# The gated sum of the experts joins the residual on two engines, and the closing norm is written anew

## What is computed

```python
combine = ...                              # [tokens, 8], two entries of a row are not zero
out = jnp.zeros_like(t)
for e in range(N_EXPERTS):
    out = out + combine[:, e:e + 1] * swiglu(t, w_gate[e], w_up[e], w_down[e])
x = x + g_f * out
# at the very end
xf * lax.rsqrt(jnp.mean(xf * xf, axis=-1, keepdims=True) + NORM_EPS) * g
```

## Time and profile before

| what | us |
|---|---|
| median of 3 runs | 1572.42 |
| range of these runs | 1570.97 to 1575.75 |
| the profiled execution, whole time | 1572.48 |
| its span on the core, from first to last instruction | 1570.7 |
| outside of the span | 1.8 |

### The profile page before, as it was taken

The page is one execution under the profiler, slowest core; times in us unless marked ns, Lnnn a source line. Parts: engine busy times, 40 slices in busy tenths (PEclk is TensorE's granted clock), DMA queues, the critical chain, the costliest instruction groups (busy, mean ns, idle before and its releaser), DMA issues.

```text
span 1570.7 us, 19868 instructions
## 1 busy us (share of the span) xinstructions
PE 1471.8 (94%) x7238; PEld 1200.2 (76%) x7239; DVE 1240.2 (79%) x1722; ACT 915.9 (58%) x1202; POOL 5.1 (0%) x17
## 2 busy tenths in 40 slices
PE   7999999997999998988899998959999999999995
PEld 5888888885788887866788887747778878877883
DVE  6767889768667888777777886795888888898887
ACT  6656564547556654465433333554776787777674
POOL 0000000000000000000000000000000000000000
PEclk9999999999999999999999998979999999999997
DMA  9654448873345467643567784312588889888882
GB/s 350 235 222 154 173 168 302 318 270 134 134 164 192 167 227 269 241 161 111 186 254 267 252 320 172 108 54 81 200 323 306 312 302 338 307 312 325 303 315 92
DMA packets 53416, 358.16 MB, mean 228 GB/s; under 512 B 6096, under 2 KB 7120, under 8 KB 12640
## 3 DMA queue, kind: packets, MB, share of 16 engines
q1 hardware_dynamic: 52736, 354.77, 60.9%
q0 software_dynamic: 176, 2.13, 0.4%
q10 hardware_dynamic: 432, 0.30, 0.1%
HBM read 356.13 MB, written 1.05 MB: 227 GB/s over the span
## 4 chain that ended last, share of the span: by engine, by line
PE 68%; DVE 17%; ACT 7%; issue 6%; DMA 1%; PEldq 0%; DVEq 0%; PEld 0%; ACTq 0%; SPq 0%
PE ps L437 21%; PE ps L439 20%; PE ps L438 20%; DVE wlo L1527 6%; ACT whi L1055 3%; PE ps L916 2%; PE ps L595 1%; DVE tok L2224 1%; PE ps L646 1%; PE ps L529 1%; DVE attn_scratch L1856 1%; DMA raw<-stream_dram 1%; DVE tok L1775 1%; ACT attn_scratch L1245 1%; DVE tok L1709 1%
## 5 line engine op out<-in xcount | busy, mean ns | idle before, releaser
L1527 DVE TENSOR_TENSOR wlo<-raw,whi 128x2048 fp32r<-128x2048 f32 (+2 forms) x304 | 651.3, 2165 | 144.1 <-ACT whi L1055 131.0
L1055 ACT ACTIVATE whi<-raw 128x2048 fp32r<-128x2048 f32 (+2 forms) x304 | 547.5, 1819 | 233.2 <-PE ps L439 228.3
L437 PE MATMUL ps<-whi,xhi 128*128 128x512 f32 (+3 forms) x1360 | 536.5, 394 | 19.5 <-DVE wlo L1527 9.4
L439 PE MATMUL ps<-whi,xlo 128*128 128x512 f32 (+3 forms) x1360 | 524.0, 385 | 0.0
L438 PE MATMUL ps<-wlo,xhi 128*128 128x512 f32 (+3 forms) x1360 | 523.8, 385 | 0.0
L437 PEld LDWEIGHTS ps<-whi,xhi 128*128 128x128 f32 x1360 | 258.2, 190 | 81.0 <-DVE wlo L1527 13.0
L439 PEld LDWEIGHTS ps<-whi,xlo 128*128 128x128 f32 x1360 | 257.9, 190 | 52.3
L438 PEld LDWEIGHTS ps<-wlo,xhi 128*128 128x128 f32 x1360 | 258.5, 190 | 47.0
L437 PE MATMUL ps<-whi,ahi 128*128 128x512 f32 x440 | 177.9, 404 | 5.2 <-DVE wlo L1527 5.1
L439 PE MATMUL ps<-whi,alo 128*128 128x512 f32 x440 | 174.1, 396 | 0.0
L438 PE MATMUL ps<-wlo,ahi 128*128 128x512 f32 x440 | 173.2, 394 | 0.0
(11 more groups left out here) (286 smaller groups left out, 1179.9 us busy)
## 6 DMA issues: line engine op xcount, KB each, us to landing
raw<-stream_dram SPq DMA_DIRECT2D x317, 1024.0 KB, 5.1
raw<-stream_dram SPq DMA_DIRECT2D x32, 512.0 KB, 4.3
attn_scratch<-toep_dram POOLq DMA_DIRECT2D x1, 2048.0 KB, 9.5
raw<-stream_dram SPq DMA_DIRECT2D x2, 528.0 KB, 4.4
h<-x_dram SPq DMA_DIRECT2D x2, 512.0 KB, 4.8
y<-tok SPq DMA_DIRECT2D x2, 512.0 KB, 2.7
head_scratch<-w_s_dram SPq DMA_DIRECT2D x1, 512.0 KB, 14.2
head_scratch<-vg_dram SPq DMA_DIRECT2D x1, 512.0 KB, 11.2
```

Of the source, the lines that this page charges most:

```text
L437: pe.matmul(o, xh, wh, start=start, stop=False)
L439: return pe.matmul(o, xl, wh, start=False, stop=stop)
L1055: act.activation(whi[:, q % SPL, 0:w], raw[:, s % RAW, 0:w], ACT.Copy).then_inc(sem("hi_done"), 1)
L1527: dve.tensor_tensor(wlo[:, q % SPL, 0:w], raw[:, s % RAW, 0:w], whi[:, q % SPL, 0:w].bitcast(F32), ALU.subtract).then_inc(sem("lo_done"), 1)
```

## The change

- POOL gets a queue behind its table. When the last residual before the experts is added (`h_added` at 14) it loads the closing norm's weights into `gates[:, 0]`, a gate's place that is free from there on. When `y_added` is at eight it multiplies `macc` by the gate and adds it to `h`, tile by tile, four instructions of 128 x 1024.
- `scatter` and `add_expert` go through the tiles outside and the halves inside, where it was the other way.
- Behind the loop `add_gated` takes the place of `add_expert`: for each tile, two instructions of 128 x 512 that make PSUM * `comb` * gate, and one of 128 x 1024 that adds this to `h`. DVE waits for POOL (`others_in`) before it.
- DVE multiplies `h` by the norm's weights while ACT squares; then one small instruction for both tiles at each step of the root; then DVE scales the left halves and ACT the right halves, and SP stores four pieces of 128 x 512.

```diff
-            sp.wait_ge(sem("y_copied"), 2 * NE + 1)
-            sp.wait_ge(sem("y_psum"), 2 * (2 * NE + 1))
-            sp.dma_start(TC[:, 0, :], fg_in.to_broadcast([P, D])).then_inc(sem("fg_landed"), 16)
             for t in range(NT):
-                sp.wait_ge(sem("y_ready"), t + 1)
-                sp.dma_start(out[0, t * P:(t + 1) * P, :], TA[:, t, :]).then_inc(sem("stored"), 16)
-            sp.wait_ge(sem("stored"), 16 * NT)
+                for n, done in enumerate(("out_left", "out_right")):
+                    sp.wait_ge(sem(done), t + 1)
+                    sp.dma_start(out[0, t * P:(t + 1) * P, n * W:(n + 1) * W], TA[:, t, n * W:(n + 1) * W]).then_inc(sem("stored"), 16)
+            sp.wait_ge(sem("stored"), 2 * 16 * NT)
...
+            g.wait_ge(sem("h_added"), 7 * NT)
+            g.dma_start(gates[:, 0, :], fg_in.to_broadcast([P, D])).then_inc(sem("fg_landed"), 16)
+            g.wait_ge(sem("y_added"), NE)
+            for t in range(NT):
+                g.tensor_tensor(macc[:, t, :], macc[:, t, :], gates[:, 1, :], ALU.mult).then_inc(sem("others_gated"), 1)
+                g.wait_ge(sem("others_gated"), t + 1)
+                g.tensor_tensor(h[:, t, :], macc[:, t, :], h[:, t, :], ALU.add).then_inc(sem("others_in"), 1)
...
-            stats(h)
+            act.activation(st[:, 26:27], ones[:, 0:1], ACT.Sqrt)
+            act.wait_ge(sem("h_added"), T.up("h_added", NT))
+            for t in range(NT):
+                act.activation(TA[:, t, :], h[:, t, :], ACT.Square, accum_out=st[:, t:t + 1]).then_inc(sem("sq"), 1)
+            act.wait_ge(sem("ms"), T.up("ms"))
+            act.activation(st[:, 4:6], st[:, 2:4], ACT.Sqrt).then_inc(sem("rms"), 1)
+            act.wait_ge(sem("end_rinv"), 1)
+            for t in range(NT):
+                act.activation(TA[:, t, W:D], macc[:, t, W:D], ACT.Copy, scale=st[:, 28 + t:29 + t]).then_inc(sem("out_right"), 1)
...
+            def add_gated(i):
+                for t in range(NT):
+                    dve.wait_ge(sem("y_psum"), T.up("x_y"))
+                    for n in range(2):
+                        c = slice(n * W, (n + 1) * W)
+                        m = dve.scalar_tensor_tensor(macc[:, t, c], ps[:, (5, 7, 3, 4)[2 * t + n], :], comb[:, t, i], gates[:, 1, c],
+                                                     ALU.mult, ALU.mult)
+                    link(m)
+                    m = dve.tensor_tensor(h[:, t, :], macc[:, t, :], h[:, t, :], ALU.add)
+                    if t:
+                        m.then_inc(sem("y_added"), 1)
...
-            add_expert(slice(NE, NE + 1))
+            dve.wait_ge(sem("others_in"), NT)
+            add_gated(slice(NE, NE + 1))
...
+            dve.wait_ge(sem("y_added"), 2 * NE + 1)
+            dve.sem_inc(sem("h_added"), NT)
+            dve.wait_ge(sem("fg_landed"), 16)
             for t in range(NT):
-                dve.wait_ge(sem("y_added"), 2 * NE + 1)
-                link(dve.tensor_tensor(macc[:, t, :], macc[:, t, :], gates[:, 1, :], ALU.mult))
-                dve.tensor_tensor(h[:, t, :], macc[:, t, :], h[:, t, :], ALU.add).then_inc(sem("h_added"), 1)
-            dve.wait_ge(sem("fg_landed"), 16)
-            normalise(h, TA, TC[:, 0, :], "y_ready")
+                m = dve.tensor_tensor(macc[:, t, :], h[:, t, :], gates[:, 0, :], ALU.mult)
+            link(m)
+            dve.wait_ge(sem("sq"), T.up("sq", NT))
+            dve.tensor_scalar(st[:, 2:4], st[:, 0:2], 1.0 / D, EPS, ALU.mult, ALU.add).then_inc(sem("ms"), 1)
+            dve.wait_ge(sem("rms"), T.up("rms"))
+            dve.reciprocal(st[:, 28:30], st[:, 4:6]).then_inc(sem("end_rinv"), 1)
+            dve.wait_ge(sem("end_rinv"), 1)
+            for t in range(NT):
+                dve.tensor_scalar(TA[:, t, 0:W], macc[:, t, 0:W], st[:, 28 + t:29 + t], None, ALU.mult).then_inc(sem("out_left"), 1)
```

More of the change, by code:

```diff
@@ L929, in scatter @@
                 pe.wait_ge(sem("y_copied"), T.up("x_y"))
-                for n in range(2):
-                    for t in range(NT):
-                        b = (5, 7, 3, 4)[2 * n + t]
+                for t in range(NT):
+                    for n in range(2):
+                        b = (5, 7, 3, 4)[2 * t + n]
                         pe.matmul(ps[:, b, :], GT[:, t, :], yhi[:, 4 * n:4 * n + 4, :], start=True, stop=False)
@@ L2218, in add_expert @@
             def add_expert(i):
-                for n in range(2):
+                for t in range(NT):
                     dve.wait_ge(sem("y_psum"), T.up("x_y"))
-                    for t in range(NT):
+                    for n in range(2):
                         o = macc[:, t, n * W:(n + 1) * W]
-                        m = dve.scalar_tensor_tensor(o, ps[:, (5, 7, 3, 4)[2 * n + t], :], comb[:, t, i], o, ALU.mult, ALU.add)
+                        m = dve.scalar_tensor_tensor(o, ps[:, (5, 7, 3, 4)[2 * t + n], :], comb[:, t, i], o, ALU.mult, ALU.add)
                 m.then_inc(sem("y_added"), 1)
+            def add_gated(i):
+                for t in range(NT):
+                    dve.wait_ge(sem("y_psum"), T.up("x_y"))
+                    for n in range(2):
+                        c = slice(n * W, (n + 1) * W)
[5 more added lines that the diff above has]
+                        m.then_inc(sem("y_added"), 1)
             T.n["xg_ready"] = 0
@@ L2271, in _ @@
                         lo_of_output()
-                        add_expert(bass.ds(i + 1, 1))
+                        add_gated(bass.ds(i + 1, 1))
                     with dve.Else():
                         dve.drain()
-                        for name, k in (("places", 1), ("dve", 2), ("xg_ready", 2), ("g_taken", 1), ("lo_done", EXP), ("x_tok", 6),
+                        for name, k in (("places", 1), ("dve", 4), ("xg_ready", 2), ("g_taken", 1), ("lo_done", EXP), ("x_tok", 6),
                                         ("x_a", 6), ("x_tr_free", 6), ("y_copied", 1), ("y_added", 1)):
@@ L2280, in _ @@
                 dve.drain()
-                dve.sem_inc(sem("dve"), 2 * NE)
+                dve.sem_inc(sem("dve"), 4 * NE)
                 dve.sem_inc(sem("y_copied"), NE)
                 dve.sem_inc(sem("y_added"), NE)
+            dve.wait_ge(sem("y_added"), 2 * NE + 1)
+            dve.sem_inc(sem("h_added"), NT)
+            dve.wait_ge(sem("fg_landed"), 16)
             for t in range(NT):
-                dve.wait_ge(sem("y_added"), 2 * NE + 1)
-                link(dve.tensor_tensor(macc[:, t, :], macc[:, t, :], gates[:, 1, :], ALU.mult))
-                dve.tensor_tensor(h[:, t, :], macc[:, t, :], h[:, t, :], ALU.add).then_inc(sem("h_added"), 1)
-            dve.wait_ge(sem("fg_landed"), 16)
-            normalise(h, TA, TC[:, 0, :], "y_ready")
+                m = dve.tensor_tensor(macc[:, t, :], h[:, t, :], gates[:, 0, :], ALU.mult)
[5 more added lines that the diff above has]
+            dve.wait_ge(sem("end_rinv"), 1)
+            for t in range(NT):
+                dve.tensor_scalar(TA[:, t, 0:W], macc[:, t, 0:W], st[:, 28 + t:29 + t], None, ALU.mult).then_inc(sem("out_left"), 1)
 _OUT = ((1, S, D), "float32")
```

2 lines of the change are left out of this document (1 added, 1 removed).

## The result

| what | before | changed |
|---|---|---|
| median of 20 runs, us | 1572.34 | 1575.49 |
| range, us | 1570.96 to 1576.48 | 1573.57 to 1579.57 |
| ratio to before, 95% interval | | 1.0021, 1.0012 to 1.003 |
| span of the profiled execution, us | 1570.7 | 1571.8 |

The change makes the kernel slower, by 3.15 us of the medians. That is clear of noise: the interval of the ratio leaves out 1. The time lies in the range of the forecast, but on the other side of the kernel before than the forecast of 1571.1.

A forecast was written before the change was run, and what follows sets the result against it. PE bounds the experts (94% busy), DVE close behind (79%); the end is one chain. From 1572.48, the end gains 3.3 and POOL's contention costs PE 1.9: 1572.48 - 3.3 + 1.9 = 1571.1 us, range 1567.5 to 1577.0.

The forecast's parts named there:

- The end: Behind the last expert, from the first half added to the span's end: shortened by 3.3 us, between 2.3 and 3.9.
- from the first half to the squares: Behind the loop: the residual is full and ACT can start squaring 5.58 us after 1554.08, at 1559.7.
- ACT's two halves: Final scaling: ACT does a 128 x 512 half in some 0.6 us, estimated from 1.14 for 128 x 1024.
- last landing: When the last output store lands: 1567.0 by one store's 2.7 us, or 1567.2 by the bytes' bound.
- The share of the load: At the end: moving SP's load of the norm's weights off the chain gives, by itself, some 2.1 us.
- GpSimd's price: POOL's four two-input instructions of 128 x 1024: 2.3 us each, 9.2 us in all, from its select.
- The upper end of 4.6: POOL's instruction takes 4.6 us, two inputs read in turn; as a rival with turns, PE loses 15.4, 1584.6 us, chance 0.10.
- That a delayed L1541 is PE's delay: Last turn: DVE's slack is 0.2 to 0.7 us, so one split delayed by 2.3 us is nearly all PE's.
- if DVE's pairs stay together: Last turn, the forecast's case: POOL uses the gaps between DVE's pairs, PE loses 1.9 us; chance 0.33.
- they take turns, one whole instruction each: Last turn, rival: POOL and DVE alternate, PE loses 6.4 us, time 1575.6, slower by 0.2%; chance 0.25.
- A and B: Last turn's first two slots made by DVE: PE starts A at 1507.32, wants B at 1510.1; DVE has B at 1509.5.
- What was costed at nothing: The norm's weights loaded shortly before 1098 us, SP's queue changes, and the other order in `scatter` and `add_expert`: 0 us.

The follow-up runs named there:

- quarters: Changed kernel with GpSimd's same work from the same moment, but in sixteen pieces of 128x256: 1570.29 us.
- halves: Changed kernel with GpSimd's work in eight pieces of 128x512, each let go by a count where DVE has other work or idle time: 1569.02 us.
- copies: Changed kernel with eight one-input GpSimd copies in place of its four instructions, the first seven experts' gated sum left out: 1570.94 us.
- memsets: Changed kernel with nine GpSimd memsets of 128x1024 in place of its four instructions, the first seven experts' gated sum left out: 1569.91 us.
- one call ahead: Changed kernel with one more GpSimd instruction of the same kind before its wait for the eighth addition, result read by nobody: 1579.07 us.

## Why the prediction was right and wrong

**The end.** Its 3.3 us (between 2.3 and 3.9) measured 2.9. The steps, as laid out: from the first half to the squares 5.58, measured 5.63; squares 2.32 and 2.37, measured 1563.72 to 1566.17, 2.45 with the step to the mean; root to scaling 0.63, measured 0.65. ACT's two halves were put at 1.2 and took 1.33. From the first store's issue to the span's end it was 4.2 by the sum and 1571.8 - 1567.33 = 4.5. There the sum had slipped: it named two bounds for the last landing, 1567.0 and 1567.2, and added the 0.4 to the earlier one; with the later one the end gives 3.1. The share of the load, 2.1, is about twice the 1.0 of the trace (the medians leave room for both): the sum looked at the last square and forgot that the first tile's root and scaling would stand behind it.

**GpSimd's price.** 2.3 us from the select's row; 2.35 measured alone. The upper end of 4.6 was not near. The rows of 4.4 and 6.6 are waiting.

**That a delayed L1541 is PE's delay** was right. The slack was 0.2 to 0.7 us, read from the earlier trace rows; of the 6.6 us by which DVE's rows were stretched (4.33, 1.25 and 1.07 at L2195) 6.4 came out at the scatter.

**The step that failed** is the choice between the two orders, "if DVE's pairs stay together". It was taken since it lay in the middle and since "only in it does neither engine push ahead of work that is already queued". Neither is a reason from a row. In the runs the two engines alternate from the second pair on: 6.4 us lost, not 1.9, and with the end's 2.9 the sign turns. The rival "they take turns, one whole instruction each" gave 6.4 and 1575.6, and 1575.49 was measured. It was right in its total and not in its path: it had GpSimd between A and B, where in truth the first pair did stay together, and it had L2195 unharmed, which lost 1.07. It had 7.9 us of PE's waits, where 5.6 were measured, since 2.1 of the loss shows as PE busy at half clock. That its time is met within 0.1 us is partly luck: its end was 0.4 too good. By the rule of the Trainium skill (SBUF — State Buffer, Who interferes with whom) one of two such instructions waits for the whole of the other; the trace agrees, with 2.25 us a turn, and so do quarters, halves, copies and memsets. The same section of the Trainium skill counts `cast` and `tensor_scalar` of one input among those that can contend, which the prediction left out; the trace agrees there too, with L2195 at 1.55 and L2207 at 2.04 us.

**What was costed at nothing** did cost nothing: with the scatter's new order and the load near 1094 us, but without GpSimd's work, the last turn is 49.0 us as before and the time 1569.11.

The chances had the measured outcome in the right class, within 0.3%, and the rival that came nearest at 0.25 beside the forecast's 0.33. The range holds the measured time because it was drawn to take in that rival, not because of the forecast's own mechanism. Forecast and rival both let the engines shut each other out; they differ in who is next, no row of before decided that, and it set the sign.

## What to carry to other kernels

Work on GpSimd that reads SBUF is not free because GpSimd is idle: here a DVE instruction with two inputs in SBUF lost up to one GpSimd instruction's length, and as PE follows DVE with half a microsecond of slack, that went to the end. So look at what DVE does in the same stretch, cut GpSimd's work to the size of DVE's slack, and let the pieces go by a count that DVE raises where it turns to PSUM or waits; here that turned +3.15 us into -3.15 with the same arithmetic. PE's waits alone do not tell what was lost: behind the wait of 3.12 us the granted clock was 0.50, and so 2.1 of the 6.4 us stood under busy time. When two orders of a queue give results of different sign, and no row decides, the sign is open until a run decides it.

## What the runs showed of the hardware

- Being shut out showed as no idle time in these profiles. It showed as a longer instruction, on both engines: 4.4 for 2.29 us on L1541, 4.4 for 2.35 on GpSimd.
- GpSimd's two-input instruction took 2.35 us for 1024 columns alone and 1.28 to 1.31 for 512.
- GpSimd's reads, of one or of two inputs, held off DVE's instructions with two SBUF inputs; its memsets did not (4.47 us for a pair). DVE's instructions of 128 x 256 with one input in PSUM kept their 0.41 to 0.43 us throughout.
- DVE instructions with one SBUF input and no PSUM can be held too: a cast of 128 x 512 took 2.04 us for 0.42, and two `tensor_scalar` of 128 x 128 took 1.55 for 0.48 beside reads and 0.83 beside memsets.
- With both queued they alternate by whole instructions, except that the first pair of L1541 passed GpSimd's first request together, in each of the kernels whose work starts at the eighth addition. It is not a first call's cost. Why is open.
- Behind PE's waits of 3.12 us (last turn) and 2.69 us (the kernel "one call ahead") rows show a granted clock of 0.50 (1514.69 to 1516.69, and 1111 to 1113), and a product every 0.43 us and not every 0.23. In the last turn this cost nothing, since DVE's next slot was not there earlier; in the other place PE's next eight products took 1.5 us more.
